# Prompt's mixing and last tiles moved behind the sample's, beside the sample's expert choice; the sample's gather ahead of the prompt's rounds; GLA's gate pieces two to a tile

## The reference

```python
h  = RMSNorm(x)
P  = h @ w_in     # GLA q,k,v,gate,codes | GQA q,k,v | zA | zB
A  = gla(P)       # 4 heads, chunks of 64, forward scan + backward scan
B  = attention(P) # 8 query heads, 2 key heads, axial rope, bidirectional
x  = x + (sigmoid(zA) * (A @ w_o_gla) + sigmoid(zB) * (B @ w_o_att)) @ w_out
h2 = RMSNorm(x)
aff = softmax(h2 @ w_router)             # 16 experts
gate, idx = top_k(aff.T, cap)            # per request group: 128 rows of the sample, 32 of the prompt
ye = ((silu(h2[idx] @ w_gate) * (h2[idx] @ w_up)) @ w_down) * gate
y  = x + scatter_add(ye at idx)
```

## Time and profile before

| | |
|---|---|
| median of three runs | 3130.28 us |
| the profiled execution | 3130.15 us, span 3128.6 us |
| mean granted TensorE clock | 0.981 of 2.4 GHz |
| instructions | 51566 |
| busy share PE / PEld / DVE / ACT / POOL | 96 / 77 / 55 / 49 / 18 % |
| HBM read / written | 522.19 / 77.33 MB, 192 GB/s over the span |

### The profile page before, as it was taken

The page is one execution under the profiler, slowest core; times in us unless marked ns, Lnnn a source line. Parts: engine busy times, 40 slices in busy tenths (PEclk is TensorE's granted clock), DMA queues, the critical chain, the costliest instruction groups (busy, mean ns, idle before and its releaser), DMA issues. The chain is left out here.

```text
span 3128.6 us, 51566 instructions
## 1 busy us (share of the span) xinstructions
PE 2991.1 (96%) x19346; PEld 2401.4 (77%) x19346; DVE 1715.3 (55%) x1759; ACT 1521.8 (49%) x1665; POOL 573.2 (18%) x729
## 2 busy tenths in 40 slices
PE   8999999999989999989958999999999999999998
PEld 6888888778778799878846777777777777777776
DVE  4100000555543599833366676676767667676765
ACT  4211111566632366622435566565666656566564
POOL 0038884012220000011101111001111100111100
PEclk9999999999999999999978999999999999999999
DMA  5323321433335100054447877787787778878772
GB/s 177 112 97 132 129 90 67 136 121 109 105 108 198 56 21 18 9 201 164 141 177 284 303 279 286 279 316 286 284 306 279 287 277 313 289 281 310 279 286 88
DMA packets 195566, 600.71 MB, mean 192 GB/s; under 512 B 14176, under 2 KB 44912, under 8 KB 195488
## 3 DMA queue, kind: packets, MB, share of 16 engines
q1 hardware_dynamic: 165312, 508.49, 44.5%
q0 software_dynamic: 21312, 73.35, 7.8%
q10 hardware_dynamic: 8864, 17.83, 1.6%
HBM read 522.19 MB, written 77.33 MB: 192 GB/s over the span
## 5 line engine op out<-in xcount | busy, mean ns | idle before, releaser
L2095 DVE TENSOR_TENSOR ex_w_lo<-ex_w_raw,ex_w_hi 128x2048 fp32r<-128x2048 f32 x384 | 875.8, 2291 | 327.7 <-ACT ex_w_hi L2048 324.2
L2048 ACT ACTIVATE ex_w_hi<-ex_w_raw 128x2048 fp32r<-128x2048 f32 x381 | 725.5, 1916 | 339.4 <-PE ex_ps_s L2180 339.3
L2180 PE MATMUL ex_ps_s<-ex_w_hi,ex_xS 128*128 128x512 f32 x2048 | 564.5, 393 | 0.0
L2180 PEld LDWEIGHTS ex_ps_s<-ex_w_hi,ex_xS 128*128 128x128 f32 x2048 | 379.9, 188 | 82.4 <-issue 6.6
L2180 PE MATMUL ex_ps_s<-ex_w_lo,ex_xS 128*128 128x512 f32 x1024 | 316.2, 390 | 0.0
L2180 PE MATMUL ex_ps_s<-ex_w_hi,ex_hidS 128*128 128x512 f32 x1024 | 290.9, 396 | 0.0
L2034 POOL DMA_INDIRECT y<-choice_then_rows,ex_rows_y x16 | 43.7, 2728 | 1122.6 <-DVE choice_then_rows L2136 1122.6
L2191 PE MATMUL ex_ps_p<-ex_w_raw,ex_xP 128*32 128x256 f32 x4096 | 229.2, 382 | 0.0
L109 PE MATMUL pj_ps_tok<-pj_w_hi,act_hl 128*128 128x512 f32 x560 | 223.1, 398 | 2.4 <-DVE act_hl L442 2.4
L2180 PEld LDWEIGHTS ex_ps_s<-ex_w_lo,ex_xS 128*128 128x128 f32 x1024 | 192.4, 188 | 40.6
L110 PE MATMUL pj_ps_tok<-pj_w_lo,act_hl 128*128 128x512 f32 x560 | 222.1, 397 | 0.0
(11 more groups left out here) (337 smaller groups left out, 5136.5 us busy)
## 6 DMA issues: line engine op xcount, KB each, us to landing
ex_w_raw<-w_e_gate SPq DMA_DIRECT2D x128, 1024.0 KB, 5.6
ex_w_raw<-w_e_up SPq DMA_DIRECT2D x128, 1024.0 KB, 10.4
ex_w_raw<-w_e_down SPq DMA_DIRECT2D x128, 1024.0 KB, 9.5
proj_t<-pj_stage SPq DMA_DIRECT2D x60, 256.0 KB, 2.0
pj_w_raw<-w_cols ACTq DMA_DIRECT2D x7, 2048.0 KB, 9.3
z_w_raw<-w_z SPq DMA_DIRECT2D x16, 512.0 KB, 4.0
gate_logits<-gl_z_stage SPq DMA_DIRECT2D x32, 256.0 KB, 2.1
pj_w_raw<-x SPq DMA_DIRECT2D x10, 512.0 KB, 3.8
```

Source lines behind the costliest of these rows:

```text
L2048: act.activation(whl[0][:, j % NHL], raw[:, j % NRAW], ACT.Copy).then_inc(w_hi, 1)
L2095: dve.tensor_tensor(whl[1][:, j % NHL], raw[:, j % NRAW], whl[0][:, j % NHL].bitcast(F32), ALU.subtract).then_inc(w_lo, 1)
L2180: mm = pe.matmul(ps_s[:, s, c:c + 512], x(part, k), whl[w][:, j % NHL, kk, c:c + 512], start=k == 0 and part + w == 0, stop=k == 2 * PU - ...
```

## The change

**Two activation tensors.** `act_hl` becomes a sample part and a prompt part (`Columns`); the prompt part stays in memory until the end of `finish_mixer`. `mix` takes the column blocks as an argument: for `ma` these are the two of the sample. `mg` still handles all three, but splits each of its input rows in two (sample, prompt).

**finish_mixer.** It is written out for all ten tiles. Buffers for x, its sum, gamma and the turned rows lie in the memory of w_out's raw form. Affinities are turned straight to the partitions of `vals`, without a DMA. The eight units of w_o_att are loaded again by SP and split on ACT and DVE. Behind sample tile 7's products PE makes the prompt's mixing (`mix_prompt`, 24 matmuls of 256 columns for each of the eight channel tiles), DVE gates it and GpSimd adds `gla_gated`. Then come the prompt's two tiles. All 16 rounds of the sample stand between these pieces on DVE, and its lists are merged to slots at the end of the phase. `choose` is gone.

**experts.** SP starts the weights at the beginning of its own block. GpSimd gathers the sample's rows at once; DVE makes the prompt's four rounds (16 rows of 256) and lists first; PE turns the sample's rows and the prompt's lists; the prompt's gather follows. In expert 0 the prompt's first pair of products stands behind sample unit 3, not ahead of unit 0.

**gla.** Gate logits are made two pieces to a tile in tiles 1 to 3, with exp, ln, log gate, running sum and centre one tile earlier or so; the backward log gate is made at the end of the head before. The backward key product goes from GpSimd to DVE behind forward update 5; both query products and `gate_low` stand behind forward update 7.

The core of the diff:

```diff
+class Columns:
+    def block(self, part, k, a, b):
+        return self.sample[:, part, k, a:b] if b <= TS else self.prompt[:, part, k, a - TS:b - TS]
...
-    for c, (a, b) in enumerate(TOK3):
+    for c, (a, b) in enumerate(blocks):
...
# mix, input rows of mg (ACT; DVE likewise)
-                        act.activation(act_hl[:, 0, k], rows[k % NR], ACT.Copy).then_inc(rows_hi, 1)
+                        act.activation(act_hl.sample[:, 0, k], rows[k % NR][:, 0:TS], ACT.Copy).then_inc(rows_hi, 1)
+                        act.activation(act_hl.prompt[:, 0, k], rows[k % NR][:, TS:T], ACT.Copy).then_inc(rows_hi, 1)
...
# gla
-        turn_at = lambda t, last: 2 * LIFT + t + (0 if last else min(max(t, 0), 2 * LIFT))
-        gate_at = lambda n: 2 * LIFT + 1 + 2 * n
+        turn_at = lambda t, last: 2 * LIFT + t + (0 if last else min(2 * t + 1, 2 * LIFT))
+        gate_at = lambda n: 2 * LIFT + 3 * (n // 2) + 2 * (n % 2)
...
-                    log_gate(i, 1)
...
-                    between = {(0, 0): lambda: q_product(i, 0), (0, 2): lambda: None if last else gate_low(i + 1), (0, 4): lambda: low(0), (0, 6): lambda: q_product(i, 1),
-                               (1, 1): lambda: None if last else low(1)}
+                    between = {(0, 3): lambda: low(0), (0, 5): lambda: k1_product(i), (0, 7): products, (1, 1): lambda: None if last else low(1)}
...
+                        logits = () if last or not 1 <= t <= LIFT else (2 * t - 2, 2 * t - 1)
...
# finish_mixer, DVE, behind tile 6
+                add_x(LAST)
+                normalise(LAST)
+                gate(0)
+                unit_low(4)
+                gate(1)
+                unit_low(5)
+                router_max(LAST)
+                affinities(LAST)
+                gate(2)
+                unit_low(6)
+                rounds(0, 1)
+                gate(3)
+                unit_low(7)
+                rounds(1, 2)
+                gate(4)
+                prompt_low(0)
+                gate(5)
+                rounds(2, 3)
+                gate(6)
+                rounds(3, 4)
+                gate(7)
+                rounds(4, 5)
+                prompt_low(1)
+                rounds(5, 9)
+                add_x(NTS)
+                rounds(9, 10)
+                normalise(NTS)
+                rounds(10, 13)
+                add_x(NTS + 1)
+                router_max(NTS)
+                rounds(13, 14)
+                normalise(NTS + 1)
+                affinities(NTS)
+                rounds(14, 16)
...
# finish_mixer, PE
+                def mix_prompt(t, ks=range(KC)):
+                    c = 512 * (t % 2)
+                    pe.wait_ge(u_lo, CR + t + 1)
+                    pe.wait_ge(x1_done, CR + LAST)
+                    pe.wait_ge(gated, CR + t - 1)
+                    for k in ks:
+                        mm = three_passes(pe, ps_x[:, 0, c:c + TP], [w[:, k] for w in att_hl[t % PAIRS]],
+                                          [act_p[:, j, k] for j in range(2)], k == 0, k == KC - 1)
+                    if ks[-1] == KC - 1:
+                        mm.then_inc(mix_full, 1)
...
+                mix_prompt(0)
+                turn_aff(LAST - 1)
+                mix_prompt(1)
+                turn_h(LAST)
+                mix_prompt(2, front)
+                router(LAST)
+                mix_prompt(2, back)
+                mix_prompt(3, front)
+                turn_aff(LAST)
+                mix_prompt(3, back)
+                for t in range(4, KC):
+                    mix_prompt(t)
+                for half in range(2):
+                    products(NTS, half)
+                products(NTS + 1, 0)
+                products(NTS + 1, 1, range(3))
+                turn_h(NTS)
+                products(NTS + 1, 1, range(3, KC))
+                router(NTS)
+                turn_h(NTS + 1)
+                turn_aff(NTS)
+                router(NTS + 1)
+                pe.wait_ge(conv, CR + 3)
+                pe.wait_ge(x1_done, CR + NTS + 1)
+                for j in range(4):
+                    tr = pe.transpose(ps_x[0:CS, 0, P * j:P * j + SAMPLE_ROWS], lists[0:SAMPLE_ROWS, j], cst["ident"][0:SAMPLE_ROWS, 0:SAMPLE_ROWS])
+                tr.then_inc(lists_tp, 1)
+                turn_aff(NTS + 1)
...
# experts, GpSimd
-                gather(0)
+                gather_rows(pool, 0, 0)
+                pool.wait_ge(slots_p, CR + 1)
+                gather_rows(pool, 0, 1)
...
# experts, SP
+                ph.start(sp)
+                start_weights(sp)
...
# experts, DVE, ahead of expert 0
+                for r in range(CP // 8):
+                    top_eight(dve, step, r, vals, lists, idx, r, prompt_rows, TP)
```

More of the change, by code:

```diff
@@ L104, in _, with __init__, tile @@
                     pool.sem_clear(range(a, b))
+class Columns:
+    def __init__(self, sample, prompt):
+        self.sample, self.prompt = sample, prompt
+    def block(self, part, k, a, b):
+        return self.sample[:, part, k, a:b] if b <= TS else self.prompt[:, part, k, a - TS:b - TS]
+    def tile(self, part, n):
+        if isinstance(n, int) and n >= NTS:
+            return self.prompt[:, part, :, (n - NTS) * P:(n - NTS + 1) * P]
+        return self.sample[:, part, :, bass.ds(n * P, P)]
 def three_passes(pe, out, a, b, first, last):
@@ L792, in attention, with mix @@
         ph.clear()
-def mix(nc, tag, act_hl, w, w_unit, z_rows, out, add=None, o=None, stored=None, source=None, rows_in=None, before=None, keys=None, follow=None, prepare=None):
+def mix(nc, tag, act_hl, w, w_unit, z_rows, out, add=None, o=None, stored=None, source=None, rows_in=None, before=None, keys=None, follow=None, prepare=None, blocks=TOK3):
     with ExitStack() as ctx:
@@ L1613, in body @@
                             turn(t - 1)
[L1614 to L1616 removed]
+                        for p in logits[1:]:
+                            gate_logits(i + 1, p // LIFT, p % LIFT, base + gate_at(p), gate_at(p) % 2)
                     z_at("end")
@@ new lines, in _ @@
+                norm(LAST)
+                unit_high(4)
+                unit_high(5)
+                h_copy(LAST)
+                aff_out(LAST - 1)
+                exp(LAST)
+                unit_high(6)
+                aff_out(LAST)
+                unit_high(7)
+                for h in range(2):
+                    prompt_high(h)
+                norm(NTS)
+                h_copy(NTS)
+                norm(NTS + 1)
+                exp(NTS)
+                aff_out(NTS)
+                h_copy(NTS + 1)
@@ L1767, in _, with rounds @@
+                def rounds(a, b):
+                    dve.wait_ge(a_out, CR + NTS)
+                    for r in range(a, b):
+                        top_eight(dve, step, r, vals, lists, idx, r, slice(0, SAMPLE_ROWS), TS // 2)
                 for u in range(NU // 2):
@@ L1810, in _, with products @@
+                dve.tensor_tensor(diff[:], a_row, b_sb[:, 1], ALU.subtract).then_inc(slot_out, 1)
+                dve.wait_ge(slot_out, CR + 5)
+                dve.tensor_tensor(diff[:], diff[:], a_first[:], ALU.mult).then_inc(slot_out, 1)
+                dve.wait_ge(slot_out, CR + 6)
+                dve.tensor_tensor(slots_i[0][:], diff[:], b_sb[:, 1], ALU.add).then_inc(slot_out, 1)
+                dve.wait_ge(slot_out, CR + 7)
             @block.tensor
             def _(pe):
-                def products(n, s, half, ks=range(KC)):
-                    if not first(n):
+                def products(n, half, ks=range(KC)):
+                    s, c = n % 2, 512 * half
+                    if 0 < n < NTS:
@@ L1936, in experts @@
-def experts(nc, late, affT, vals, lists, idx, h2, y, w_gate, w_up, w_down, slots_i, slots_g, slots_q, cst):
+                for n in range(LAST):
+                    products(n + 1, 0)
+                    if n > 0:
+                        turn_aff(n - 1)
+                    products(n + 1, 1, range(3))
+                    turn_h(n)
+                    products(n + 1, 1, range(3, KC))
+                    router(n)
+                mix_prompt(0)
+                turn_aff(LAST - 1)
+                mix_prompt(1)
@@ L1939, in experts @@
+        ph.clear()
+def experts(nc, late, vals, lists, idx, offset, h2, y, w_gate, w_up, w_down, slots_i, slots_g, slots_q, cst):
     with ExitStack() as ctx:
@@ L2023, in body @@
                         pool.wait_ge(turned, CR + XT + TURNS * e)
-                        gather(e + 1)
+                        for j in range(2):
+                            gather_rows(pool, e + 1, j)
                     for j, src in enumerate(slots_g):
```

586 lines of the change are left out of this document (323 added, 263 removed).

## The result

The changed kernel took 3112.85 us (median of five), against 3130.28 us before; the ratio is 0.9941, with a 95% interval of 0.9929 to 0.9953. Measured a second time it took 3110.31 us, ratio 0.9933 (0.992 to 0.9945). So it is faster by 17 to 21 us, where I forecast 27.6. Its first profiled execution took 4316.5 us at a mean clock of 0.651, and one of nine of a later variant 15422 us, and the ratios leave both out. The profile read here is that of the second measurement (3112.27 us, span 3110.7).

The account below looks back on a forecast made before the run. The prediction took TensorE, busy 96% of the span, to bound the kernel. Its seven terms sum to -27.6 us, which takes 3130.15 us to 3102.6 us; the range is 3094 to 3118.

Parts of the forecast that it names:

- Term 1: Mixing: 192 prompt matmuls leave the attention mixing and fill TensorE's wait behind sample tile 7; -22.5 us, bounds -18 and -23.
- Term 2: From T (tile 6's router logits finished) to E (last slot of the choice written): +1.5 us, bounds -3 and +8.
- Term 3: From E to the first sample matmul of the experts, expected at E+17.6: +3.8 us, bounds 0 and +8.
- Terms 4 and 5: Expert 0: slow start at the lower clock, +0.9 us; wait for the prompt's gathered rows, +0.5 us (0 to +4).
- Term 6: Rows of the first mixing: each of eight becomes two splits on ScalarE and DVE; +1.0 us, bounds 0 and +2.
- Term 7: GLA stage: fewer waits for states, full clock in update windows, less cost of logit pieces; -12.8 us, bounds -17 and -3.
- The waits for states: GLA: of 13.0 us of TensorE waits for the chain of states 2.5 remain; -10.5 us.
- two logit pieces in a tile, +1.3, by estimate: GLA: making two gate logit pieces per tile gives ScalarE more in tiles 1 to 3; +1.3 us.
- the uncovered products: GLA: TensorE waits at each head's first backward update for query products and gate weights; 3140 us, chance 0.04.
- the rows behind all the weights: Experts' start: engines serve 12 weight units before the sample's rows, first matmul 26 us later; 3129 us, chance 0.04.
- DVE's chain longer: T to E: some 25 handovers between TensorE and DVE at 0.5 us each, E 12 us later; 3115 us, chance 0.12.
- Nothing from GLA: GLA stage: the waits are only moved, no gain; 3115 us, chance 0.08.

Follow-up runs that it names:

- the run with splits in idle stretches: Changed kernel with the splits of attention weights in tiles 3 to 6 moved behind the norm, ahead of the router's maximum: 3104.49 us, ratio 0.9917.
- the run with late loads: The four edits, plus loads of the prompt's gate logits and first three attention weight units started behind token tiles 0 and 1: 3091.98 us, ratio 0.988.
- the run with rows first: Changed kernel with the sample's turned rows copied and split ahead of expert weight units that they need not wait for: 3107.33 us, ratio 0.9928.
- the run with one unit ahead: As the run with late loads, but only the first expert weight unit started ahead of the sample's rows: 3095.4 us, ratio 0.989.
- the four edits: Changed kernel with one gate piece to a tile, splits in idle stretches, rows first and eight expert weight units held: 3092.61 us, ratio 0.9878.
- one piece to a tile: Changed kernel with GLA's gate logits again one piece to a tile, its other GLA moves kept: 3107.22 us, ratio 0.9918.
- all weights held: As the run with rows first, with all twelve expert weight units also held until the sample's rows have landed: 3109.06 us in one run.

## Why the forecast was right, and where its steps failed

The direction and the range were right (3094 to 3118). The size was not: 17.9 us in the profiled executions for 27.6. By the steps:

- **Term 1, the mixing (-22.5):** -23.5. Right. PE was never short of transfers there.
- **Term 2, T to E (+1.5):** +2.5 in the profiled execution, and -0.3 to -0.5 in the other five profiles of the same code. DVE's work was counted right (56.9 for 57.3 us). What failed is "tile 7's norm done at T+6.5", and with it "rounds from T+15.5". The split of an attention unit ahead of tile 7's sum was not in the steps, so the norm is done at T+8.2, PE stands 2.36 us, and its clock falls: rounds from T+20.6 here, from some T+17.8 in the others. Only the run with splits in idle stretches has the norm at T+6.5, and then rounds from T+14.6. That E came near T+71.2 all the same is partly luck: from the first round to E it took 51.5 to 51.6 us in every profile, where my steps have 55.7, and these 4 us cover the late rounds.
- **Not costed at all (+5.0, 115.1 to 118.6 us in the other profiles for 108.6 to 110.2 before):** the tiles ahead of T. I put the eight attention units' splits, their loads and the sigmoid of the prompt's gate logits at nothing, and named only the four splits behind T. The splits stood ahead of the next tile's sum (0.7 us in each of three tiles, 2.0 in all); the run with splits in idle stretches shows that. The sigmoid made tile 2 longer by 1.4 us, and the longer tile moved with it in the run with late loads. The first tile takes the rest, +1.3 here. Its normed rows start 21.0 us behind the stage's first matmul, 18.2 before, and 18.2 and 18.4 with late loads; so the 2.5 MB of loads at the stage's start are the cause, by two profiles and not by a median.
- **Term 3, E to the first sample matmul (+3.8):** +5.1. "The rows land near E+9.9" was E+12.3. The gather took 9.47 us, and it is the weights in flight that double it. The interleaving, "each waits for the other's next piece", was right; the run with rows first starts 3.2 us sooner behind E and shows that it needn't be.
- **Terms 4 and 5 (+1.4):** +2.5 for expert 0. Its 95.1 us are 4.1 above the 91.0 of a later expert, more than the 3 that I had named as a sign of being wrong, but 1.6 of these stood there before the change. The slow start lasted 3.8 us and cost 1.9, where I had 2.5. The wait for the prompt's rows was 1.2 us for 0.5 (0.4 and 1.8 in two other profiles); the rest was not taken apart. The prompt's gather took 2.36 us to issue beside a VectorE split (1639.12); my row said 2.65. Where VectorE stood idle, in the run with one unit ahead, it took 0.91. By the Trainium skill (SBUF — State Buffer, "Who interferes with whom") a tensor_tensor should leave the writing of descriptors alone; the measured times speak against that inference for this gather. What in the issue is slower they don't show.
- **Term 6, two splits for a row (+1.0):** about right, though the sum of `mg` and attention hides it. From `mg`'s first matmul to the attention's first scores it took 127.7 us (126.8 on the mean of ten profiles with the new input rows), 125.7 before (125.7 to 125.9 in three). The attention behind it, for which I forecast nothing, took 284.9 us for 288.0 (288.0 to 288.6 in the three profiles with the old input rows, 284.9 to 285.6 in nine of the ten with the new ones). Why, no run shows; it is 3 us of luck.
- **Term 7, GLA (-12.8):** -8.4 at the stage's end in the profiled execution, -9.6 there in the run with this stage alone, -12.5 by that run's medians. "The waits for states" (-10.5) were -11.6, the clock came back as I said, and "two logit pieces in a tile, +1.3, by estimate" failed. They leave PE without these pieces from tile 4 on, and its waits for GpSimd's sum and gating grow by 5.6 us: 3.4 to 5.5 us by the two kernels that differ in the pieces. I had asked what they add in tiles 1 to 3, and not what they leave behind.

Of the rivals, the uncovered products and the rows behind all the weights did not happen: no wait at the updates is beyond 0.6 us, and the rows came long before unit 12. "DVE's chain longer" put E 12 us late; it was 1, or none. "Nothing from GLA" falls with the run of that stage alone.

What stays open: why the four edits give 17.7 us together and 14.1 summed by their medians, and how far the medians of separate measurements (spread 3 to 6 us) can settle terms of 2 us.

## What to carry to other kernels

When filler work leaves a stretch, cost the stretch that it leaves as well as the one that it enters: the pieces of GLA's gate logits were what hid another engine's product. Put work that nobody waits for behind the result that somebody does, inside the idle time of its own queue; a split of 1.2 us ahead of a sum cost 0.7 us three times, and the fourth time it cost the clock and 3 us, in one profile 6. Before a stretch of one profile is named as the cause, look at the same stretch in every other profile that has its code: here that halved one effect and moved another from the loads to a sigmoid. The change with the four edits took 3092.6 us, and 3092.0 with the late loads, 1.2% below the kernel before.

## What the runs showed of the hardware

A gather of 128 rows took 4.46 us from issue to landing with no weights in flight, 6.13 with one 1 MB unit, 9.31 to 9.47 with four (three profiles) and 9.30 to 9.47 with twelve (five profiles). That is not a wait behind all that was asked for earlier: twelve units take some 30 us at the 2.56 us of the earlier trace rows. The Trainium skill (DMA: Bandwidth & Descriptors, "SWDGE vs HWDGE vs iDMA") says that each DMA engine has separate queues for the two kinds of transfers and goes round between them, and the trace agrees for the twelve units.

TensorE's clock fell to its lower level (0.50 in the windows of 1 us, 1.2 of 2.4 GHz) behind a wait of 2.36 or 2.37 us, at the eight transposes that follow it or just behind them, in all six profiles that have this wait. It stayed there for some 3 us in five of them and for 10 in the sixth, with the same code. It stayed at 1.00 after waits of up to 1.13 us in the same stage of the version with four edits. The length of a wait does not settle it: behind the 3.59 us at the start of `finish_mixer` the changed kernel ran at 0.50 at once, and the kernels with one piece to a tile, with the old GLA stage and with all weights held ran at 1.00 for 20 us and more.
